# Windowed attention of the first dilation group: 32-row strips against two key tiles each, tokens in natural order, values token by token

## The reference, cut to what matters

```python
A_GROUPS = ((128, 1), (512, 4), (2048, 16))      # window, dilation
A_HEADS, HEAD_DIM, S = 8, 128, 512

def mixer_dilated(qkv, qn_g, kn_g, ang):
    qkv = qkv.reshape(Bn, S, 3, N_A_GROUPS, A_HEADS, HEAD_DIM)
    q = rmsnorm(qkv[:, :, 0], qn_g[:, None, :])
    k = rmsnorm(qkv[:, :, 1], kn_g[:, None, :])
    v = qkv[:, :, 2]
    q = apply_rope(q, ang) * (HEAD_DIM ** -0.5)
    k = apply_rope(k, ang)
    for g, (window, dilation) in enumerate(A_GROUPS):
        o_g, l_g = dilated_window_attention(q[:, :, g], k[:, :, g], v[:, :, g], window, dilation)
    ...
    w = jax.nn.softmax(jnp.stack(lses, axis=2), axis=2)
    o = jnp.sum(w[..., None].astype(o.dtype) * o, axis=2)
    return o.reshape(Bn, S, A_W)
```

## Time and profile before

| | |
|---|---|
| runs | 3315.97, 3313.26, 3315.20 us; median 3315.2 |
| profiled execution | 3312.4 us, of which 3310.6 us span of the instructions |
| granted TensorE clock over the span | 0.999 of full speed |
| PE busy | 3265.1 us of 3310.6 |
| PEld, DVE, ACT, POOL busy | 2726.0, 1454.0, 1371.5, 1478.4 us |
| the layer's stretch with attention tiles | 2412 to 2860 us of the span |

### The profile page before, as it was taken

The page is one execution under the profiler, slowest core; times in us unless marked ns, Lnnn a source line. Parts: engine busy times, 40 slices in busy tenths (PEclk is TensorE's granted clock), DMA queues, the critical chain, the costliest instruction groups (busy, mean ns, idle before and its releaser), DMA issues. The chain is left out here.

```text
span 3310.6 us, 45311 instructions
## 1 busy us (share of the span) xinstructions
PE 3265.1 (99%) x16390; PEld 2726.0 (82%) x16390; DVE 1454.0 (44%) x2431; ACT 1371.5 (41%) x2201; POOL 1478.4 (45%) x1109
## 2 busy tenths in 40 slices
PE   9999999999999999999999999999999999999999
PEld 7888887888888888888788888887888888887777
DVE  4421476642204722136776222274465266235643
ACT  4322455542224522234655222265355255445553
POOL 4554444245543555444414554445453454354423
PEclk9999999999999999999999999999999999999999
DMA  4422222022222222222212322232221221232111
GB/s 177 146 95 95 90 79 69 28 91 98 95 95 83 96 95 95 99 92 83 70 33 69 103 95 96 88 137 96 77 71 64 77 83 64 77 133 78 59 56 64
DMA packets 78200, 289.14 MB, mean 87 GB/s; under 512 B 8672, under 2 KB 8800, under 8 KB 76896
## 3 DMA queue, kind: packets, MB, share of 16 engines
q1 hardware_dynamic: 76176, 275.77, 24.9%
q10 hardware_dynamic: 1872, 11.27, 0.9%
HBM read 280.72 MB, written 6.29 MB: 87 GB/s over the span
## 5 line engine op out<-in xcount | busy, mean ns | idle before, releaser
L622 POOL TENSOR_TENSOR w_lo<-raw,w_hi 128x512 fp32r<-128x512 f32 x1026 | 1382.4, 1370 | 1572.3 <-ACT w_hi L691 1572.1
L2144 PE MATMUL ps<-x_hi,w_hi 128*128 128x512 f32 x2536 | 1011.0, 399 | 2.2 <-DVE x_lo L1954 1.2
L2146 PE MATMUL ps<-x_hi,w_lo 128*128 128x512 f32 x2536 | 987.9, 390 | 0.0
L2145 PE MATMUL ps<-x_lo,w_hi 128*128 128x512 f32 x2536 | 987.2, 389 | 0.0
L691 ACT ACTIVATE w_hi<-raw 128x1024 fp32r<-128x1024 f32 x514 | 541.6, 1056 | 958.0 <-PE ps L2146 488.2
L2144 PEld LDWEIGHTS ps<-x_hi,w_hi 128*128 128x128 f32 x2536 | 476.3, 188 | 110.1 <-issue 11.5
L2145 PEld LDWEIGHTS ps<-x_lo,w_hi 128*128 128x128 f32 x2536 | 476.4, 188 | 104.0 <-issue 8.4
L2146 PEld LDWEIGHTS ps<-x_hi,w_lo 128*128 128x128 f32 x2536 | 476.0, 188 | 100.8
L1427 DVE TENSOR_TENSOR T<-T,ps 128x512 f32<-128x512 f32 x66 | 45.4, 688 | 470.2 <-PE ps L2146 465.2
L642 POOL TENSOR_TENSOR square_parts<-T,square_parts 128x512 fp32r<-128x512 f32 (+1 forms) x71 | 87.8, 1238 | 238.5 <-ACT square_parts L1069 238.5
L2280 PE MATMUL ps<-h_hi,w_hi 128*128 128x512 f32 (+1 forms) x440 | 153.2, 348 | 0.0
(11 more groups left out here) (381 smaller groups left out, 5129.4 us busy)
## 6 DMA issues: line engine op xcount, KB each, us to landing
raw<-in_weights SPq DMA_DIRECT2D x514, 512.0 KB, 3.3
Y<-in_x_t SPq DMA_DIRECT2D x4, 512.0 KB, 6.7
mem_split<-norm_hi ACTq DMA_DIRECT2D x2, 1024.0 KB, 3.9
mem_split<-norm_lo ACTq DMA_DIRECT2D x2, 1024.0 KB, 5.9
mem_hi<-mem_split ACTq DMA_DIRECT2D x2, 1024.0 KB, 7.5
mem_lo<-mem_split ACTq DMA_DIRECT2D x2, 1024.0 KB, 10.6
out_t<-Y SPq DMA_DIRECT2D x8, 256.0 KB, 2.0
mem<-in_mem_t SPq DMA_DIRECT2D x1, 1024.0 KB, 13.4
```

Source lines behind the costliest of these rows:

```text
L622: ins = pool.tensor_tensor(g.wl[:, k, part], g.raw[:, k, part], g.wh[:, k, part], ALU.subtract)
L2144: mm(out, wh[:, c], xh[:, kc, :], start=kc == 0, stop=False)
L2145: mm(out, wh[:, c], xl[:, kc, :], start=False, stop=False)
L2146: ins = mm(out, wl[:, c], xh[:, kc, :], start=False, stop=kc == DC - 1)
```

## The change

- The tokens stay in natural order. The sort in the last FFN goes (silu and product write in order; the 8 DVE copies and 8 ACT copies of Y are gone). The tables, masks and the host's output follow.
- `a_v` units of groups 1 and 2 take their stationary tokens with a step of 4 (`by_class`).
- `qk_apply` reads its product from T in natural order and writes it in class order with a step of 4 on the reading side, the queries turned by 16 places in two pieces (`ROWS`, `TURN`). Group 0's keys stay in natural order.
- With the turn, 32 query rows of a class have all their group-0 keys in two neighbouring key tiles. Scores of group 0 are now four strips of 32 rows, each with its own 32 stationary columns and 256 key columns, written to its own 32 PSUM partitions. The tile has 512 columns of scores, one bank, double-buffered (banks 4 and 5). Masks, exponentials and copies are 512 wide.
- The values are turned around: probabilities stationary, values moving, output queries by features. Groups 1 and 2 are one full matmul each; group 0 is eight matmuls with 32 stationary columns. The probabilities are not scaled; DVE scales the 128 x 128 result into `OT`, PE transposes it one step later, and DVE writes it to `O` in token order. A half therefore has 19 steps instead of 18.

Parts of the diff (the rest follows from these):

```diff
-        g.MASK = over("masks", (P, NT, 768), BF16, 72)
+        g.MASK = over("masks", (P, NT, S), BF16, 72)
+        g.OT = over("o_rows", (P, 2, P), F32, 76)
...
-                groups = [Group(E_A + 16 * half, 16, k) for k in range(18)]
+                groups = [Group(E_A + 16 * half, 16, k) for k in range(19)]
...
-ATT_WIDTH = {"mem": N_MEM, "a": 768, "b": S}
+ATT_WIDTH = {"mem": N_MEM, "a": S, "b": S}
...
+TURN = 16
+ROWS = ((slice(0, P - TURN), slice(TURN, P)), (slice(P - TURN, P), slice(0, TURN)))
+
+
+def prob_a(flat_t, e):
+
+    at = 1024 + S * (e % 2)
+    return flat_t[:, at:at + ATT_WIDTH[att_kind(e)[0]]]
+
+
+def out_a(g, e):
+    return g.ps[:, 7, e % 2 * P:(e % 2 + 1) * P]
+
+
+def turned_a(g, e):
+    return g.ps[:, 7, (2 + e % 2) * P:(3 + e % 2) * P]
...
-        if c == 3:
-            for j in range(DC):
-                act.wait_ge(s.sort_in, j + 1)
-                fn(g.Y[:, j, :], g.T[:, 4 + j % 2, :], ACT.Copy).then_inc(s.sort_out, 1)
...
-            fn(flat_t[:, 2560:2560 + width], flat[:, 6 * S:6 * S + width], ACT.Copy).then_inc(s.ptc_done, 1)
+            fn(flat_t[:, 2048:2048 + width], flat[:, 6 * S:6 * S + width], ACT.Copy).then_inc(s.ptc_done, 1)
...
+        x = g.T[:, 5 + r % 2, :] if r < R_MEM[1] else normed(g, r)
...
+        if roped(r) and r < R_MEM[1]:
+            raw, part = g.T[:, 5 + r % 2, :], (r - R_A) % 6
+            if part == 1:
+                v.tensor_tensor(x, raw, rstd, ALU.mult).then_inc(s.qk_done, 1)
+            else:
+                for to, of in ROWS if part % 2 == 0 else ((slice(0, P), slice(0, P)),):
+                    ins = v.tensor_tensor(rows_of(x)[:, :, to], classes(raw)[:, :, of], classes(rstd)[:, :, of],
+                                          ALU.mult)
+                ins.then_inc(s.qk_done, 1)
+        elif roped(r):
...
+            if windowed:
                 dve.wait_ge(s.pt_mm, e - 1)
-                v.tensor_tensor_reduce(buf, flat[:, 4 * S:4 * S + width], g.MASK[:, c, :], -1.0, -2 * MASKED, ALU.add,
+                v.tensor_tensor_reduce(buf, ps[:, 4 + e % 2, 0:width], g.MASK[:, c, :], -1.0, -2 * MASKED, ALU.add,
                                        ALU.min, nb).then_inc(s.smax_done, 1)
             else:
                 v.tensor_reduce(nb, ps[:, 4 + e % 2, 0:width], AX.X, ALU.max, negate=True).then_inc(s.smax_done, 1)
-        if k >= 2:
-            kind, _, _ = att_kind(e - 2)
-            dve.wait_ge(s.o_mm2, e - 1)
-            v.tensor_copy(out_of(e - 2), ps[:, 5, 256:384] if kind == "a" else ps[:, 7, 0:P]).then_inc(s.o_done, 1)
+        if 2 <= k <= n + 1:
+            f = e - 2
+            dve.wait_ge(s.o_mm2, f + 1)
+            if windowed:
+                dve.wait_ge(s.pn_done, f + 1)
+                if f - E_A >= 2:
+                    dve.wait_ge(s.ot_mm, f - E_A - 1)
+                v.tensor_scalar(g.OT[:, f % 2, :], out_a(g, f), g.small[:, 10, f % 4:f % 4 + 1], None, ALU.mult)\
+                    .then_inc(s.on_done, 1)
...
+        if windowed and k >= 3:
+            f = e - 3
+            _, hd, c = att_kind(f)
+            dve.wait_ge(s.ot_mm, f - E_A + 1)
+            for rows, tokens in ROWS:
+                ins = v.tensor_copy(classes(g.O[:, hd, :])[:, c, tokens], turned_a(g, f)[:, rows])
+            ins.then_inc(s.o_done, 1)
         if k < n:
             dve.wait_ge(s.p_done, e + 1)
-            link(v.reciprocal(den, den))
-            v.tensor_scalar(buf, buf, den, None, ALU.mult).then_inc(s.pn_done, 1)
+            if windowed:
+                v.reciprocal(den, den).then_inc(s.pn_done, 1)
...
-            pe.wait_ge(s.pn_done, e + 1)
+            pe.wait_ge(s.p_done if windowed else s.pn_done, e + 1)
             if e:
                 pe.wait_ge(s.ptc_done, e)
             if e == E_A:
                 pe.wait_ge(s.o_done, E_A)
-            at = 1024 + 768 * (e % 2)
+            p = prob_a(flat_t, e)
             for b in range(ATT_WIDTH[att_kind(e)[0]] // P):
-                ins = nc.tensor.transpose(flat[:, 6 * S + b * P:6 * S + (b + 1) * P],
-                                          flat_t[:, at + b * P:at + (b + 1) * P], ident)
+                ins = nc.tensor.transpose(flat[:, 6 * S + b * P:6 * S + (b + 1) * P], p[:, b * P:(b + 1) * P], ident)
             ins.then_inc(s.pt_mm, 1)
-        if k >= 2:
+        if windowed and k >= 3:
+
+            f = e0 + k - 3
+            pe.wait_ge(s.on_done, f - E_A + 1)
+            pe.wait_ge(s.o_done, f)
+            nc.tensor.transpose(turned_a(g, f), g.OT[:, f % 2, :], ident).then_inc(s.ot_mm, 1)
...
-            if kind == "a" and k <= n:
-                pe.wait_ge(s.smax_done, e + 2)
-            out = ps[:, 5, 256:384] if kind == "a" else ps[:, 7, 0:P]
-            blocks = values(e)
-            for b, blk in enumerate(blocks):
-                ins = mm(out, blk, flat_t[:, 2560 + b * P:2560 + (b + 1) * P], start=b == 0,
-                         stop=b == len(blocks) - 1)
-            ins.then_inc(s.o_mm2, 1)
+            if windowed:
+                window_values(e)
...
+    def window_scores(e):
+
+        _, hd, c = att_kind(e)
+        qk, out = g.QR[:, hd % 2, :, :], ps[:, 4 + e % 2, :]
+        pe.wait_ge(s.qk_done, R_A + 6 * (hd + 1))
+        pe.wait_ge(s.p_done, E_A)
+        pe.wait_ge(s.smax_done, e - 1)
+        for b in range(NT):
+            rows, q = slice(32 * b, 32 * b + 32), qk[:, 0, c * P + 32 * b:c * P + 32 * b + 32]
+            if b < NT - 1:
+                mm(out[rows, 0:2 * P], q, qk[:, 1, b * P:(b + 2) * P], start=True, stop=True)
+            else:
+                mm(out[rows, 0:P], q, qk[:, 1, natural[b]], start=True, stop=True)
+                mm(out[rows, P:2 * P], q, qk[:, 1, natural[0]], start=True, stop=True)
+        mm(out[:, 2 * P:3 * P], qk[:, 2, natural[c]], qk[:, 3, natural[c]], start=True, stop=True)
+        mm(out[:, 3 * P:4 * P], qk[:, 4, natural[c]], qk[:, 5, natural[c]], start=True, stop=True).then_inc(s.s_mm, 1)
+
+    def window_values(e):
+
+        _, hd, c = att_kind(e)
+        cols, out = natural[hd % 4], out_a(g, e)
+        pe.wait_ge(s.vcopy_done, V_A + 12 * (hd // 4 + 1))
+        pe.wait_ge(s.ptc_done, e + 1)
+        if (e - E_A) % 16 == 0:
+            pe.wait_ge(s.o_done, e)
+        for grp in (1, 2):
+            at = 2048 + (grp + 1) * P
+            mm(out, flat_t[:, at:at + P], g.VV[:, grp, c, cols], start=grp == 1, stop=False, skip_group_check=True)
+        for near in range(2):
+            for b in range(NT):
+                at = 2048 + near * P + 32 * b
+                ins = mm(out[32 * b:32 * b + 32, :], flat_t[:, at:at + 32], g.VV[:, 0, (b + near) % NT, cols],
+                         start=False, stop=near == 1, skip_group_check=True)
+        ins.then_inc(s.o_mm2, 1)
...
-                value_unit(op.u, op.t % 4, 2, S, g.XH, g.XL, natural, range(4), op.mid,
+                value_unit(op.u, op.t % 4, 2, S, g.XH, g.XL, by_class if grp else natural, range(4), op.mid,
...
+    row = np.arange(P)[:, None]
+    i = (row + TURN) % P
+    out = np.zeros((P, NT, S), np.float32)
+    keys = (row // 32 * P + np.arange(2 * P)[None]) % S
     for c in range(NT):
-        out[:, c, 0:S] = np.where(abs(c + 4 * i - CLASS_ORDER[None]) <= 64, 0, MASKED)
+        out[:, c, 0:2 * P] = np.where(abs(c + 4 * i - keys) <= 64, 0, MASKED)```

PE's rows at one step, before (the tile of an `a_qk` unit in the middle of half 0, after the unit's last matmul; the `group()` step is L2737 to L2768, `waits` are semaphores):

```order
L2146 MATMUL ps<-x_hi,w_lo 128x512
L2737 MATMUL ps<-mat,T 128x128 [waits ptc_done,pn_done]
L2737 MATMUL ps<-mat,T 128x128 x5
L2754 MATMUL ps<-T,v_tok 128x128 [waits o_done,smax_done,ptc_done,vcopy_done]
L2754 MATMUL ps<-T,v_tok 128x128 x5
L2768 MATMUL ps<-qk 128x512 [waits smax_done,p_done,qk_done]
L2768 MATMUL ps<-qk 128x128 x2
L2144 MATMUL ps<-x_hi,w_hi 128x512 [waits lo_ready,vcopy_done,qraw_done]
```

More of the change, by code:

```diff
@@ L1111, in group @@
             width = ATT_WIDTH[kind]
-            buf = flat_t[:, 1024 + 768 * (e % 2):1024 + 768 * (e % 2) + width]
+            buf, den = prob_a(flat_t, e), e % (4 if kind == "a" else 2)
             act.wait_ge(s.smax_done, e + 1)
@@ L1450, in ffn @@
             pair(i)
-        if c == 3:
-            for j in range(DC):
-                if j >= 2:
-                    dve.wait_ge(s.sort_out, j - 1)
-                v.tensor_copy(rows_of(g.T[:, 4 + j % 2, :]), classes(g.Y[:, j, :])).then_inc(s.sort_in, 1)
-            dve.wait_ge(s.sort_out, DC)
         def write(j, half=None):
@@ L2670, in pe_program @@
     natural = [slice(c * P, (c + 1) * P) for c in range(NT)]
+    by_class = [slice(c, S, NT) for c in range(NT)]
     def scores(e):
         kind, hd, c = att_kind(e)
-        if kind == "a":
-            qk = g.QR[:, hd % 2, :, :]
-            return [(qk[:, 0, natural[c]], qk[:, 1, :], 0, S),
-                    (qk[:, 2, natural[c]], qk[:, 3, natural[c]], S, P),
```

(51 more changed lines are left out.)

58 lines of the change are left out of this document (23 added, 35 removed).

## The result

The changed kernel takes 3297.5 us (median of 5 runs, 3295.92 to 3298.15). The runs of the kernel before that stood beside it gave 3315.2 us (5 runs, 3313.26 to 3315.97): ratio 0.995, 95% interval 0.994 to 0.996. The forecast was 3295.7. Later runs of the kernel before had lower medians, 3313.2 to 3313.5 us (9 to 27 runs each), so against them the gain is some 16 us and not 17.7.

A forecast was written before the change was run, and what follows sets the result against it. PE was taken to bound the kernel: 18.0 us from steps less width changes, plus 1.5 of waits, takes 19.5 off the profiled 3312.4, giving 3292.9; the median, 2.8 above, is 3295.7 us. Range for 8 in 10: 3286 to 3311.

The forecast's parts named there:

- The step: One attention step of PE, transposes through scores: 2.69 us against 3.30, 0.61 saved, times 32 tiles 19.5 us.
- the width change: PE going from full width to strips and back: 0.38 us a pair, one pair a step, 4 more pairs costing 1.5 us.
- The closely spaced steps: Four steps half an `a_v` unit apart: PE's wait for DVE before the transposes goes, 1.5 us saved.
- What is late next is PE itself: At the closely spaced steps: DVE's chain done near 2555.8, PE asking from 2556.80, so PE no longer waits.
- The strided tokens: 384 `a_v` matmuls of groups 1 and 2: weight loads with a 16-byte step stay hidden, 0; bounds 0 to 85 us.
- rival C: Strided loads bound the 16 `a_v` units of groups 1 and 2 from about 0.227 us; fourfold loads: 3381 us; chance 0.08.
- About 0.15 us more: DVE's `qk_apply` product (0.67 us): cost of a second short instruction for three of six tiles.
- Nothing: Effect of the changed DVE and ACT work on the kernel's time, PE waiting for `qk_done` one unit later.
- The sort: Removing 8 DVE and 8 ACT copies under the last FFN's out phase gives 0.
- the turned output (D): Rival: PE waits anew for DVE's scaling before transposing the output, 0.28 us in 32 steps: 3304.7 us; chance 0.08.
- A: Rival: only two strips run at a time, step 3.53 us, 0.23 above before: 3322.6 us; chance 0.10.
- B: Rival: four strips at three times single file, 0.28 us more a step: 3304.7 us; chance 0.12.

The follow-up runs named there:

- both pairs of traces: Changed kernel against itself with plain `a_v` slices (3295.3 us); kernel before against itself with step 4 in groups 1 and 2's `a_v` (3316.3 us).
- the kernel with both losses removed: Changed kernel with plain slices in all `a_v` units and the plain one-piece `qk_apply` product for all groups: 3292.7 us, ratio 0.9938.

## Why the prediction came out

The time lies 1.8 us above the forecast, within the uncertainty of the comparison. The main mechanism was right: four strips run side by side. But several sizes were off and partly cancelled, and two terms that were put at nothing were not nothing.

- **The step.** Forecast 0.61 us saved, measured 0.65; four strips side by side, 0.43 + 0.43, held to within 0.03. The difference is the width change, 0.38 forecast, 0.33 measured. 32 x 0.65 less 4 x 0.33 is 19.5, where the forecast had 18.0.
- **The closely spaced steps.** 1.5 us forecast; 4 x 0.43 by the two traces. Steps and waits would make 21.2; the kernel with both losses removed shows 20.5 in its layer. Most of the 0.7 between them is one step, where PE now waits for DVE's rotary embedding: it takes 3.27 us in that kernel too, 0.6 more than the others. "What is late next is PE itself" held at the closely spaced steps, but the prediction asked the question nowhere else.
- **The strided tokens: the term that failed.** The prediction took 0 from "it may double to 0.224 and still be hidden". By the estimate above the load did about double, to 0.229, and 384 matmuls came 8 ns later each: 3.1 us, as both pairs of traces have it inside the layer, where the medians show 2.2 and 2.9. The bounds (0 to 85) held. The failed step is "still be hidden": a load of 0.229 beside rival C's threshold of 0.227 would be just past it, but the step of 2 cost 6 ns a matmul with a load far below the threshold, so that threshold is not the rule either.
- **DVE: also failed.** "About 0.15 us more" for the product was 0.41 to 0.54, since only the added instruction was counted and not the step in the operand. "Nothing" was 0.8 us of PE's time. The new short instructions at each tile took 340, 346 and 188 ns and not some 0.2 to 0.28 us; PE doesn't wait for them. The row that could have warned is DVE's copy with this very step, 726 ns in the earlier trace rows. It was set beside a two-operand pass, 669 ns, and looked harmless; a copy between the same buffers without the step, one instruction in the same stretch of the trace of before, took 426 (another, within T, took 1036, so the pair is a hint and no price):

```profile
L1319 DVE COPY T<-Y 128x512 f32<-128x512 f32 x1 | 0.4, 426 | 0.0
```

- **The sort, the turned output (D)**: nothing, as forecast. **A and B** fall by the spacing of the strips (3.85 times one stream, where B had 3.0 to 3.2); A's price was confirmed to 5% where its condition was made true.
- **The median before.** The forecast was made against 3315.2. With 3313.4 from later runs, its 19.5 us would have meant 3293.9, and the gain of 16 is 3.5 us short of it. The near hit is in part luck: a high median before hid half of what the mechanism lost.

In sum: 20.5 of steps and waits, less 3.1 for strided weights, less 0.8 for DVE's product: 16.6 us inside the layer, and some 0.4 less outside the span.

## What to carry to other kernels

Matmuls on 32-column parts ran four at a time here, fp32 records included, so where PE is the bound, masked or banded attention can be computed only where it counts; put all strips of a step next to each other, since the way out and back costs as much as three records of 128 columns (0.33 us). An operand's step cost time on both engines that read it here, TensorE's weight loads and DVE: price it from a row with the same step beside a row of the same operation without it, and don't put it at nothing because something longer runs over it. And when PE's work between two of DVE's chains gets shorter, look at every place where DVE had been ready only just in time.

## What the runs showed of the hardware

- Column parts behave as queues of their own: the other order of the value strips made no difference (0.1 us in the median), and a later record of one part starts before earlier ones of another (2506.91 and 2507.00 us). Eight 128-column matmuls take 1.77, 0.90 and 0.46 us in one, two and four parts.
- Going from full width to 32-column parts and back costs 0.33 us.
- A weight load of 128 x 128 fp32 shows 188, 194, 311 and 332 ns in the trace for steps of 1, 2, 4 and 8 elements, and 512-column matmuls behind it come every 227, 233, 235 to 237 and 247 ns.
- DVE's two-operand product over 512 fp32 columns takes 668 ns plain and 1079 to 1082 with a step of four on the SBUF operand, whether or not the PSUM operand has it too; its one-operand copy with that step takes 724.
- One DMA issue on ACT's queue, the same in every kernel, took between 0.50 and 1.98 us.
